# Attention's background product and the branch products in another orientation: weights stationary, 512 and 256 tokens moving, and merged rows kept feature by token

## The chip, the cores and the metric

The kernel runs on one core of one Trainium2 chip. The metric is device time in microseconds (us), the median of several executions. The engines are named as in the profile: PE (TensorE, with its weight loads as PEld), ACT (ScalarE), DVE (VectorE), POOL (GpSimd) and SP (SyncE, which here only issues DMAs).

## What is computed

Two sequences (512 and 256 tokens, width 1024) go through two layers and a last RMSNorm. The kernel treats them as 768 tokens, six tiles of 128. The reference, cut to what matters:

```python
def layer(x, ...):
    h = rmsnorm(x, norm_g)
    proj = h @ w_in
    qa, ka, va, gfl, gbl, za, qb, kb, vb, zb, ma, mb = jnp.split(proj, split_points(), axis=-1)
    ya = gla_branch(qa, ka, va, gfl, gbl, za, ..., w_branch_a)   # (o * silu(za)) @ w_branch_a
    yb = attn_branch(qb, kb, vb, zb, ..., w_branch_b)            # (o * silu(zb)) @ w_branch_b
    merged = jax.nn.sigmoid(ma) * ya + jax.nn.sigmoid(mb) * yb
    return x + merged @ w_out
```

`ma`, `mb`, `ya`, `yb` and `merged` are all 768 x 1024. The change touches these five alone.

## The kernel before

Every dense product runs in three passes of type fp32r: each operand is split into a high part and a low part, and PE adds high x high, high x low and low x high in PSUM. A contraction of 1024 is eight blocks of 128 (`KT` = 8, index `k`). Weights come block by block through a ring of four slots: SP loads `w_raw`, ACT writes the high part `w_hi` (`split`, L992), POOL writes the low part `w_lo` (L1460), and PE waits for `w_lo_done` before a block and signals `w_used` after it. ACT splits three blocks ahead. PE's program is written out by hand, and semaphores order the engines.

The stages of a layer that matter here, in PE's order:

1. **Attention** (`attention_group`), four groups of 20 steps. A step `n` turns the probabilities of one unit on PE (four transposes, `turn_p`, L838), issues the scores of unit `n + 2` (L827, L828), sometimes the product with the values (L852, L853), and turns of queries (L813) in three steps of a group: 3, 6 and 8, in the first group 3, 6 and 11. After such a step `turn_p` waits for `q_stack`, which ACT (L1178) and DVE (L1859) set once both parts of these queries are written. The rest of the step is filled by `background`: pieces of `h @ w_in` for `ma` and `mb`. One group does two pieces of 256 output columns, 16 blocks of 6 token tiles, so 96 tiles (`BG_TILES`). The table `ATT_TILES` says how many tiles each step takes, and `ATT_DONE` is its running sum. One tile is three matmuls with 128 tokens of `act` stationary and 256 columns of the weights moving (L635 to L637). Results stand in banks 5 to 7. ACT copies them to `stg` (L1007) and stores them to the DRAM tensor `proj`.
2. **Four branch products** (`gemm_tokens`, with `three_passes`, L589 to L591): `w_branch_a` with columns 0 to 511, then 512 to 1023, and `w_branch_b` likewise. Each is 8 blocks x 6 token tiles x 3 matmuls = 144 matmuls with 128 tokens stationary and 512 weight columns moving. Token tile `t` has bank `t`. A product takes along six turns (`turn_step`, four transposes of 128x128 and a wait for a free bank 6 or 7, L719). In the first they are of `va`, in the second and third of `zb`, in the fourth of the first half of `merged`.
3. **Merging**: DVE multiplies each bank with the sigmoid factor (`merge`, L1790), and for branch B adds both branches (L1795). The factors come from `proj` by `fetch`, and ACT applies the sigmoid. The sum has tokens on the partitions, but the output product wants features there. So PE turns `merged`, ACT copies the high part out of PSUM into `o_hi` (`turn_hi`, L1049), and DVE writes the low part `o_lo` (`turn_lo`, L1625).
4. **Output product** (`gemm_output`), twice 144 matmuls of the same form for tokens 0 to 383 and 384 to 767. The first takes along the six turns of the second half of `merged`, and waits at block `k` = 4 until they are written.

Of the kernel before, what the change touches and what calls it, by code (L numbers as in the profile page):

```python
# [33 lines left out]
F32 = mybir.dt.float32  # L34
# [6 lines left out]
P = 128  # L41
# [73 lines left out]
ATT_DONE = [[first + sum(tiles[:n + 1]) for n in range(GROUP * UNITS)] for first, tiles in zip(ATT_FIRST, ATT_TILES)]  # L115
ATT_PIECE = [done.index(KT * NT) for done in ATT_DONE]
# [106 lines left out]
class Semaphores:  # L223


    def __init__(self, nc):
# [72 lines left out]
        self.merged_ready = sem("merged_ready")  # L299
        self.zb_ready = sem("zb_ready")  # L300
# [28 lines left out]
def trunk(nc, x_prompt, x_sample, norm_g, w_in, w_gate_f, b_gate_f, w_gate_b, b_gate_b, gla_norm_g,  # L329
# [33 lines left out]
    ma = sb("ma", [P, NT, D], R_ACT)  # L363
    zb = sb("zb", [P, NT, D], R_ACT + NT * D * 4)
    mb = sb("mb", [P, NT, D], R_ACT + NT * D * 4)
    b_lo = sb("b_lo", [P, NT, D], R_M, F32R)
    merged = sb("merged", [P, NT, D], R_V)
# [101 lines left out]
    with nc.Block() as block:  # L469

        @block.sync
        def _(sp):
# [15 lines left out]

            def fetch_inputs(layer, c):
# [17 lines left out]
            def fetch_ma(k):  # L507

                if k == 0:
                    sp.wait_ge(s.stored, at.peek("stored", NBG * 16))  # L510
                if k < 4:
                    fetch(ma, J_MA + k, k * BGW, D, s.m_in[k // 2])

            def fetch_mb(layer, k):
# [3 lines left out]
                if k < 4:  # L518
                    fetch(mb, J_MB + k, k * BGW, D, s.m_in[k // 2])
# [64 lines left out]
        def _(pe):  # L584
# [8 lines left out]
            def gemm_tokens(a_hi, a_lo, turns=None, first=0, half_free=True, after=None, enter=None):  # L593


                for k in range(KT):
                    pe.wait_ge(s.w_lo_done, at("w_lo_done"))
                    if k == KT // 2 and not half_free:
                        pe.wait_ge(s.turn_free, at.peek("turn_free", 2))
                    for t in range(NT):  # L600
                        if k == 0:
                            pe.wait_ge(s.drained, at.peek("drained", t + 1 - NT))
                            if enter:
                                enter(t)
# [4 lines left out]
                        if turns and first <= k < first + 3 and t in (2, NT - 1) and (k, t) != (KT - 1, NT - 1):  # L609
                            turns(2 * (k - first) + t // 3)  # L610
                    (last if k < KT - 1 else pe.drain()).then_inc(s.w_used, 1)
                    if after:
                        after(k)
                at.skip("drained", NT)

            def background(start, stop, bank0=BG_BANK, spare=0, ends=False, turned=0):


                for u in range(start, stop):
# [20 lines left out]
                    elif ends and k == KT - 1 and t % 2 == 1:  # L640
                        last.then_inc(s.bg_done, 1)

# [79 lines left out]

            def merged_step(half):

                def step(t):
                    pe.wait_ge(s.merged_ready, at("merged_ready"))
# [1332 lines left out]
```

## Time and profile before

| what | value |
|---|---|
| median of 3 runs | 1930.85 us (1930.23 to 1932.38) |
| the profiled execution's own time | 1933.38 us |
| its span, first to last instruction | 1931.0 us |
| PE busy | 1882.5 us, 97% of the span |
| DVE, ACT, POOL busy | 987.7, 944.0, 682.8 us (51%, 49%, 35%) |
| granted PE clock | 0.997 of full speed over the span |

A busy PE is not PE at its peak: a matmul's duration as printed (289 ns for 256 columns) reaches past the start of the next. What one matmul costs in a row of them is the distance from its start to the start of the next, which the timeline shows.

### The profile page before, as it was taken

What the parts mean: (1) busy time and instruction counts of PE and PEld (TensorE: products, weight loads), DVE (VectorE), ACT (ScalarE), POOL (GpSimd) and SP (SyncE); (2) the same over time, 40 slices, a digit from 0 to 9 for tenths busy, and PEclk for the clock granted to TensorE, in tenths of its full rate; (3) what the DMA queues carried; (4) which work ended last, traced back from release to release, by engine and by line L of the source; (5) the groups of instructions that cost most, each with busy time, mean ns of one, the idle gap of its engine ahead of it and who ended that gap; (6) DMA issues with size and microseconds to landing.
All of it is one profiled execution on the core that took longest, in us unless ns stands there. A gap on an engine that the chain in (4) does not pass through costs nothing.

```text
span 1931.0 us, 38149 instructions
## 1 busy us (share of the span) xinstructions
PE 1882.5 (97%) x14864; PEld 1728.9 (90%) x14864; DVE 987.7 (51%) x1376; ACT 944.0 (49%) x1891; POOL 682.8 (35%) x688
## 2 busy tenths in 40 slices
PE   6999999999999999999999999999999999999997
PEld 6989999999999999888899899999999999988886
DVE  5113566669655554443241145657886655543324
ACT  4214555532776675423441245555337766763334
POOL 3433233258222122424653333222771221232244
PEclk9999999999999999999999999999999999999999
DMA  5322222522112114332432122225221121261323
GB/s 177 85 58 59 72 78 61 180 82 59 56 48 66 47 50 152 130 126 71 134 104 71 47 65 75 66 76 181 79 58 45 47 67 53 67 208 60 126 93 142
DMA packets 122988, 169.90 MB, mean 88 GB/s; under 512 B 15696, under 2 KB 89296, under 8 KB 122832
## 3 DMA queue, kind: packets, MB, share of 16 engines
q1 hardware_dynamic: 110880, 135.83, 23.7%
q10 hardware_dynamic: 11952, 31.86, 4.3%
q8 instruction: 113, 1.85, 0.4%
q14 instruction: 43, 0.35, 0.1%
HBM read 136.19 MB, written 31.46 MB: 87 GB/s over the span
## 4 chain that ended last, share of the span: by engine, by line
PE 89%; DVE 4%; ACT 3%; issue 3%; ACTq 1%; DMA 0%; POOL 0%; DVEq 0%
PE ps L635 12%; PE ps L636 12%; PE ps L637 12%; PE ps L589 11%; PE ps L591 11%; PE ps L590 11%; PE ps L799 4%; PE ps L838 3%; PE ps L719 2%; PE ps L852 2%; PE ps L853 2%; PE ps L827 2%; PE ps L784 2%; PE ps L828 2%; PE ps L766 1%
## 5 line engine op out<-in xcount | busy, mean ns | idle before, releaser
L1460 POOL TENSOR_TENSOR w_lo<-w_raw,w_hi 128x256 fp32r<-128x256 f32 (+1 forms) x560 | 581.4, 1045 | 1203.9 <-ACT w_hi L992 1202.8
L635 PE MATMUL ps<-w_hi,act_hi 128*128 128x256 f32 x2112 | 610.3, 289 | 6.5 <-ACT stg L1007 5.3
L637 PE MATMUL ps<-w_hi,act_lo 128*128 128x256 f32 x2112 | 597.2, 283 | 0.0
L636 PE MATMUL ps<-w_lo,act_hi 128*128 128x256 f32 x2112 | 597.1, 283 | 0.0
L992 ACT ACTIVATE w_hi<-w_raw 128x256 fp32r<-128x256 f32 (+1 forms) x560 | 273.5, 495 | 507.2 <-PE ps L591 284.2
L635 PEld LDWEIGHTS ps<-w_hi,act_hi 128*128 128x128 f32 x2112 | 403.8, 191 | 14.7 <-issue 9.6
L636 PEld LDWEIGHTS ps<-w_lo,act_hi 128*128 128x128 f32 x2112 | 404.4, 191 | 2.2
L637 PEld LDWEIGHTS ps<-w_hi,act_lo 128*128 128x128 f32 x2112 | 404.2, 191 | 0.0
L1868 DVE TENSOR_REDUCE st<-ps 128x1 f32<-128x512 f32 (+1 forms) x160 | 109.9, 691 | 126.6 <-PE ps L828 126.1
L589 PE MATMUL ps<-w_hi,o_hi 128*128 128x512 f32 x384 | 154.5, 402 | 1.7 <-DVE mb L1790 0.5
L591 PE MATMUL ps<-w_hi,o_lo 128*128 128x512 f32 x384 | 150.2, 391 | 0.0
L590 PE MATMUL ps<-w_lo,o_hi 128*128 128x512 f32 x384 | 149.8, 390 | 0.0
L1188 ACT ACTIVATE pr<-ps,st 128x512 f32<-128x512 f32 (+1 forms) x192 | 117.2, 612 | 12.0 <-DVE st L1868 9.7
L1874 DVE TENSOR_TENSOR pt_lo<-ps,pt_hi 128x512 fp32r<-128x512 f32 x128 | 88.2, 689 | 60.5 <-ACT pt_hi L1198 59.1
L1109 ACT ACTIVATE scaled<-scaled 128x768 f32<-128x768 f32 x64 | 53.2, 831 | 119.7 <-DVE scaled L1726 116.8
L1198 ACT ACTIVATE pt_hi<-ps 128x512 fp32r<-128x512 f32 x128 | 76.6, 599 | 65.9 <-PE ps L853 51.4
L838 PE MATMUL ps<-ident,pr 128*128 128x128 f32 x640 | 96.7, 273 | 7.8 <-DVE q_hl L1859 7.0
L1742 DVE COPY_PREDICATED amat<-mask,ps 128x768 f32<-128x768 uint8 x56 | 58.2, 1040 | 60.7 <-issue 48.3
L589 PEld LDWEIGHTS ps<-w_hi,o_hi 128*128 128x128 f32 x384 | 72.2, 188 | 19.1 <-issue 3.6
L589 PE MATMUL ps<-act_hi,w_hi 128*128 128x384 f32 x256 | 86.2, 337 | 0.5 <-DVE qk_t L1671 0.5
L591 PEld LDWEIGHTS ps<-w_hi,o_lo 128*128 128x128 f32 x384 | 72.1, 188 | 15.6
L591 PE MATMUL ps<-act_hi,w_lo 128*128 128x384 f32 x256 | 85.6, 334 | 0.0
(183 smaller groups left out, 3383.9 us busy)
## 6 DMA issues: line engine op xcount, KB each, us to landing
w_raw<-in_w_in SPq DMA_DIRECT2D x352, 128.0 KB, 2.1
proj<-stg ACTq DMA_DIRECT2D x36, 768.0 KB, 3.5
w_raw<-in_w_in SPq DMA_DIRECT2D x80, 256.0 KB, 2.7
w_raw<-in_w_out SPq DMA_DIRECT2D x64, 256.0 KB, 2.6
w_raw<-in_w_branch_a SPq DMA_DIRECT2D x32, 256.0 KB, 3.0
w_raw<-in_w_branch_b SPq DMA_DIRECT2D x32, 256.0 KB, 2.6
q<-proj SPq DMA_DIRECT2D x8, 768.0 KB, 8.8
zb<-proj SPq DMA_DIRECT2D x8, 768.0 KB, 9.5
```

The source lines that it names most:

```text
L589: mm(out, s_hi, m_hi, start=first, stop=False)
L590: mm(out, s_hi, m_lo, start=False, stop=False)
L591: return mm(out, s_lo, m_hi, start=False, stop=last)
L635: mm(out, act_hi[:, k, tok], w_hi[:, k % RING, 0:BGW], start=(k == 0 and t % 2 == 0), stop=False, skip_group_check=True)
L636: mm(out, act_hi[:, k, tok], w_lo[:, k % RING, 0:BGW], start=False, stop=False, skip_group_check=True)
L637: last = mm(out, act_lo[:, k, tok], w_hi[:, k % RING, 0:BGW], start=False, stop=(k == KT - 1), skip_group_check=True)
L838: last = nc.tensor.transpose(bank(pt_bank(n))[:, place * P:(place + 1) * P], pr[:, n % 2, j * P:(j + 1) * P], ident[:])
L992: A(w_hi[:, slot, 0:width], w_raw[:, slot, 0:width], ACT.Copy).then_inc(s.w_hi_done, 1)
L1188: last = A(pr[:, n % 2, i * w:(i + 1) * w], ps[:, n % 2 * HALF + i * w:n % 2 * HALF + (i + 1) * w], ACT.Exp, bias=nmax(n, i), accum_out=de ...
L1460: G.tensor_tensor(w_lo[:, slot, 0:width], w_raw[:, slot, 0:width], w_hi[:, slot, 0:width].bitcast(F32), ALU.subtract).then_inc(s.w_lo_done, 1)
L1868: V.tensor_reduce(out, view_ps(n % 2 * HALF, (HALF // k, k), (1, HALF // k)), AX.X, ALU.max, negate=True).then_inc(s.neg_max, 1)
L1874: V.tensor_tensor(p_turned(n, True), src, p_turned(n, False).bitcast(F32), ALU.subtract).then_inc(s.pt_lo_ready, 1)
```

## The change

Three things move.

- The attention background becomes `gate_background`. For each block two chunks of 128 weight columns are stationary, and the 768 tokens move. The six places of 256 PSUM columns remain, now (chunk, 256 tokens). Places 0 and 1, and places 4 and 5, lie in one bank and belong to one chunk, and are one matmul of 512 columns where they fall in one step. `ATT_DONE` is moved by one where a step would end inside such a pair.
- The branch products become `gemm_branch`: per block four chunks of 128 weight columns stationary, for each chunk one matmul group of 512 tokens and one of 256. Two chunks share three banks.
- `ma`, `mb` and `merged` are kept feature by token. So the turns of `merged` fall away. ACT makes `o_hi` and DVE `o_lo` straight from `merged` in SBUF (`merged_high`, `merged_low`), and PE waits for `merged_lo` at blocks 0 and 4 of the first output product. The fetches of `ma` and `mb` move one contiguous run of 6 KB per partition (`fetch_features`).

```diff
+ATT_DONE = [[u + (u % NT in (1, 5)) for u in done] for done in ATT_DONE]
...
-    ma = sb("ma", [P, NT, D], R_ACT)
+    ma = sb("ma", [P, KT, TOK], R_ACT)
...
+            def gate_background(start, stop):
+                u = start
+                while u < stop:
+                    i, t = divmod(u, NT)
+                    k = i % KT
+                    n = 2 if t in (0, 4) and u + 2 <= stop else 1
+                    if t == 0:
+                        pe.wait_ge(s.w_lo_done, at("w_lo_done"))
+                    if k == 0 and t % 2 == 0:
+                        pe.wait_ge(s.bg_free, at.peek("bg_free", 1))
+                        at.skip("bg_free", 1)
+                    out = ps[:, BG_BANK * HALF + t * BGW:BG_BANK * HALF + (t + n) * BGW]
+                    col = slice(t // 3 * P, (t // 3 + 1) * P)
+                    tok = slice(t % 3 * BGW, (t % 3 + n) * BGW)
+
+                    mm(out, w_hi[:, k % RING, col], act_hi[:, k, tok], start=(k == 0 and t % 2 == 0), stop=False, skip_group_check=True)
+                    mm(out, w_hi[:, k % RING, col], act_lo[:, k, tok], start=False, stop=False, skip_group_check=True)
+                    last = mm(out, w_lo[:, k % RING, col], act_hi[:, k, tok], start=False, stop=(k == KT - 1), skip_group_check=True)
+                    t += n
+                    u += n
...
+            def gemm_branch(m_hi, m_lo, turns=None, first=0, half_free=True, after=None, enter=None):
+                pieces = [(c, piece) for c in range(4) for piece in range(2)]
+                for k in range(KT):
+                    pe.wait_ge(s.w_lo_done, at("w_lo_done"))
...
+                    for c, piece in pieces:
+                        at0 = piece * (HALF if c % 2 == 0 else BGW)
+                        n = HALF if piece == c % 2 else BGW
+                        flat = c * TOK + at0
+                        b = flat // HALF
+                        opens = flat % HALF == 0
+                        if k == 0 and opens:
+                            pe.wait_ge(s.drained, at.peek("drained", b + 1 - NT))
...
+                        out = ps[:, flat:flat + n]
+                        col = slice(c * P, (c + 1) * P)
+                        mm(out, w_hi[:, k % RING, col], m_hi(k, at0, n), start=(k == 0 and opens), stop=False, skip_group_check=True)
+                        mm(out, w_hi[:, k % RING, col], m_lo(k, at0, n), start=False, stop=False, skip_group_check=True)
+                        last = mm(out, w_lo[:, k % RING, col], m_hi(k, at0, n), start=False, stop=(k == KT - 1), skip_group_check=True)
...
+                        if turns and first <= k < first + 3 and piece == 1 and c % 2 == 1:
+                            turns(2 * (k - first) + c // 2)
...
-                    if first == 0 and k == KT // 2 and c == 0:
-                        pe.wait_ge(s.turn_free, at.peek("turn_free", 2))
+                    if first == 0 and k % (KT // 2) == 0 and c == 0:
+                        pe.wait_ge(s.merged_lo, at("merged_lo", NT))
...
+                b_parts = ((lambda k, at0, n: b_hi[k // (KT // 2)][:, k % (KT // 2), at0:at0 + n]),
+                           (lambda k, at0, n: view(b_lo, at0 // P * D + k * P, (D, n // P), (1, P))))
...
-                gemm_tokens(*b_parts, half_of(zb, 1), half_free=False)
-                gemm_tokens(*b_parts, merged_step(0), first=1)
-                pe.wait_ge(s.turn_free, at.peek("turn_free", 2))
...
+                gemm_branch(*b_parts, half_of(zb, 1), half_free=False)
+                gemm_branch(*b_parts)
+
+                gemm_output(0, OUT_BANKS[0], OUT_FREE[0], lambda i: None)
...
+            def merged_high(half, b):
+                act.wait_ge(s.merged_ready, at("merged_ready"))
+                start = half * (NT * HALF) + b * HALF
+                A(view(o_hi, start, (1, HALF)), view(merged, start, (1, HALF)), ACT.Copy).then_inc(s.merged_hi, 1)
...
-                    if i < NT:
-                        turn_hi(o_hi, i, i, 4)
+                    if 1 <= i <= NT:
+                        merged_high(1, i - 1)
...
+            def merged_low(g):
+                for b in range(NT):
+                    start = g * (NT * HALF) + b * HALF
+                    dve.wait_ge(s.merged_hi, at("merged_hi"))
+                    V.tensor_tensor(view(o_lo, start, (1, HALF)), view(merged, start, (1, HALF)),
+                                    view(o_hi, start, (1, HALF)).bitcast(F32), ALU.subtract).then_inc(s.merged_lo, 1)
```

On PE, step 0 of the second attention group, four background tiles between the scores (L828, now L879) and the next turn of probabilities (L838, now L889). In a row the moving tile stands first behind the arrow, and the columns of the output last. Before:

```order
L828 MATMUL ps<-k_ll,q_hl 128x512
L635 MATMUL ps<-w_hi,act_hi 128x256
L636 MATMUL ps<-w_lo,act_hi 128x256
L637 MATMUL ps<-w_hi,act_lo 128x256
L635 MATMUL ps<-w_hi,act_hi 128x256
L636 MATMUL ps<-w_lo,act_hi 128x256
L637 MATMUL ps<-w_hi,act_lo 128x256
L635 MATMUL ps<-w_hi,act_hi 128x256
L636 MATMUL ps<-w_lo,act_hi 128x256
L637 MATMUL ps<-w_hi,act_lo 128x256
L635 MATMUL ps<-w_hi,act_hi 128x256
L636 MATMUL ps<-w_lo,act_hi 128x256
```

Now:

```order
L879 MATMUL ps<-k_ll,q_hl 128x512
L659 MATMUL ps<-act_hi,w_hi 128x512
L660 MATMUL ps<-act_lo,w_hi 128x512
L661 MATMUL ps<-act_hi,w_lo 128x512
L659 MATMUL ps<-act_hi,w_hi 128x256
L660 MATMUL ps<-act_lo,w_hi 128x256
L661 MATMUL ps<-act_hi,w_lo 128x256
L659 MATMUL ps<-act_hi,w_hi 128x256
L660 MATMUL ps<-act_lo,w_hi 128x256
L661 MATMUL ps<-act_hi,w_lo 128x256
L889 MATMUL ps<-ident,pr 128x128 x4
```

Twelve matmuls of 256 columns became three of 512 and six of 256; the columns are the same.

On PE inside a branch product, before in the fourth around a turn of `merged` (L719), from one token tile to the next:

```order
L589 MATMUL ps<-w_hi,b_hi_66 128x512
L590 MATMUL ps<-w_lo,b_hi_66 128x512
L591 MATMUL ps<-w_hi,b_lo 128x512
L719 MATMUL ps<-ident,merged 128x128 x4
L589 MATMUL ps<-w_hi,b_hi_66 128x512
L590 MATMUL ps<-w_lo,b_hi_66 128x512
L591 MATMUL ps<-w_hi,b_lo 128x512
```

Now, in the second, around a turn of `zb` (L777), which remains:

```order
L777 MATMUL ps<-ident,zb 128x128 x4
L689 MATMUL ps<-o_hi,w_hi 128x512
L690 MATMUL ps<-o_lo,w_hi 128x512
L691 MATMUL ps<-o_hi,w_lo 128x512
L689 MATMUL ps<-o_hi,w_hi 128x256
L690 MATMUL ps<-o_lo,w_hi 128x256
L691 MATMUL ps<-o_hi,w_lo 128x256
L689 MATMUL ps<-o_hi,w_hi 128x256
L690 MATMUL ps<-o_lo,w_hi 128x256
L691 MATMUL ps<-o_hi,w_lo 128x256
L689 MATMUL ps<-o_hi,w_hi 128x512
```

The turns of `merged` have no successor, the others stand twice a block as before, and a block of 18 matmuls has become one of 24.

## Rows read from the trace of the kernel before

**Rows 1.** The page: busy time of each engine, share of the span, instructions

```profile
PE 1882.5 (97%) x14864; PEld 1728.9 (90%) x14864; DVE 987.7 (51%) x1376; ACT 944.0 (49%) x1891; POOL 682.8 (35%) x688
```

**Rows 2.** Windows, layer 0: attention, branch products; PE, PEld, DVE, ACT, POOL, clock, DMA

```profile
497.10:755.40 258.30, 253.75 (x2002) 242.59 (x2001) 148.95 (x251) 183.39 (x448) 52.77 (x70) 1.00 0.18 54
755.40:899.40 144.00, 143.15 (x673) 117.22 (x672) 53.26 (x71) 54.42 (x73) 47.99 (x33) 1.00 0.41 135
```

**Rows 3.** Timeline of PE, 12 matmuls of background in attention: start, duration in us

```profile
559.95 0.28 PE L635 MATMUL ps<-w_hi,act_hi 128*128 128x256 f32 x1
...
561.27 0.28 PE L637 MATMUL ps<-w_hi,act_lo 128*128 128x256 f32 x1
```

**Rows 4.** Timeline of PE, ten matmuls with 512 weight columns moving

```profile
1102.26 0.39 PE L590 MATMUL ps<-w_lo,act_hi 128*128 128x512 f32 x1
...
1104.30 0.39 PE L590 MATMUL ps<-w_lo,act_hi 128*128 128x512 f32 x1
```

**Rows 5.** Timeline of PE, eight matmuls, weights stationary, 384 tokens moving

```profile
51.96 0.33 PE L589 MATMUL ps<-act_hi,w_hi 128*128 128x384 f32 x1
...
53.18 0.33 PE L590 MATMUL ps<-act_lo,w_hi 128*128 128x384 f32 x1
```

**Rows 6.** Timeline of PE, first and last matmul of four products of 144

```profile
97.09 0.47 PE L589 MATMUL ps<-w_hi,act_hi 128*128 128x512 f32 x1 [0.26 <-DVE qk_t L1949]
129.98 0.39 PE L591 MATMUL ps<-w_hi,act_lo 128*128 128x512 f32 x1
...
863.67 0.47 PE L589 MATMUL ps<-w_hi,b_hi 128*128 128x512 f32 x1 [0.26 <-DVE mb L1790]
899.06 0.39 PE L591 MATMUL ps<-w_hi,b_lo 128*128 128x512 f32 x1
...
1850.52 0.47 PE L589 MATMUL ps<-w_hi,o_hi 128*128 128x512 f32 x1 [0.26 <-DVE mb L1790]
1886.31 0.39 PE L591 MATMUL ps<-w_hi,o_lo 128*128 128x512 f32 x1
1886.81 0.49 PE L589 MATMUL ps<-w_hi,o_hi 128*128 128x512 f32 x1
1919.78 0.40 PE L591 MATMUL ps<-w_hi,o_lo 128*128 128x512 f32 x1
```

**Rows 7.** Timeline, second group: turns after steps 3 and 6, and DVE's queries

```profile
569.53 0.28 PE L637 MATMUL ps<-w_hi,act_lo 128*128 128x256 f32 x1
570.37 0.63 PE L838 MATMUL ps<-ident,pr 128*128 128x128 f32 x4 [0.55 <-DVE q_hl L1859]
...
578.24 0.28 PE L637 MATMUL ps<-w_hi,act_lo 128*128 128x256 f32 x1
578.51 0.30 PE L838 MATMUL ps<-ident,pr 128*128 128x128 f32 x1
...
569.36 0.86 DVE L1859 TENSOR_TENSOR q_hl<-ps,q_hl 64x256 fp32r<-64x256 f32 x2
```

**Rows 8.** Timeline of PE, first group: the turns of steps 4 and 19, values in 10

```profile
508.06 0.63 PE L838 MATMUL ps<-ident,pr 128*128 128x128 f32 x4 [0.20 <-DVE q_hl L1859]
...
525.82 0.36 PE L852 MATMUL ps<-ps_hi,v_hl 128*128 128x256 f32 x1 [0.15 <-DVE q L1883]
...
547.40 0.66 PE L838 MATMUL ps<-ident,pr 128*128 128x128 f32 x4 [0.29 <-ACTq L1190]
```

**Rows 9.** Timeline, starts of output products: DVE's products and sums, POOL's low parts

```profile
896.16 4.02 DVE L1790 TENSOR_TENSOR mb<-ps,mb 128x512 f32<-128x512 f32 x6 [11.70 <-PE ps L591]
900.10 5.88 DVE L1795 TENSOR_TENSOR merged<-merged,mb 128x512 f32<-128x512 f32 x6
...
1854.51 1.73 POOL L1460 TENSOR_TENSOR w_lo<-w_raw,w_hi 128x512 fp32r<-128x512 f32 x1 [1.77 <-ACT w_hi L992]
1857.03 1.29 POOL L1460 TENSOR_TENSOR w_lo<-w_raw,w_hi 128x512 fp32r<-128x512 f32 x1 [0.79 <-ACT w_hi L992]
```

**Rows 10.** Line L784, small products in GLA: duration ns min/median/max

```profile
L784 PE MATMUL ps<-scaled x2304: 191/197/270, 184.2 to 1328.9; 128*32 128x32 f32 x160, 128*64 128x64 f32 x32
```

More of the change, by code:

```diff
@@ L299, in __init__ @@
         self.merged_ready = sem("merged_ready")
+        self.merged_hi = sem("merged_hi")
+        self.merged_lo = sem("merged_lo")
         self.zb_ready = sem("zb_ready")
@@ L591, in three_passes, with gemm_tokens @@
                 return mm(out, s_lo, m_hi, start=False, stop=last)
-            def gemm_tokens(a_hi, a_lo, turns=None, first=0, half_free=True, after=None, enter=None):
+            def gemm_tokens(a_hi, a_lo, after):
                 for k in range(KT):
                     pe.wait_ge(s.w_lo_done, at("w_lo_done"))
-                    if k == KT // 2 and not half_free:
-                        pe.wait_ge(s.turn_free, at.peek("turn_free", 2))
                     for t in range(NT):
@@ L608, in gemm_tokens, with background @@
                             last.then_inc(s.gemm_ready, 1)
-                        if turns and first <= k < first + 3 and t in (2, NT - 1) and (k, t) != (KT - 1, NT - 1):
-                            turns(2 * (k - first) + t // 3)
                     (last if k < KT - 1 else pe.drain()).then_inc(s.w_used, 1)
-                    if after:
-                        after(k)
+                    after(k)
                 at.skip("drained", NT)
-            def background(start, stop, bank0=BG_BANK, spare=0, ends=False, turned=0):
+            def background(start, stop, bank0=BG_BANK, spare=0, turned=0):
                 for u in range(start, stop):
@@ L639, in background @@
                         last.then_inc(s.w_used, 1)
-                    elif ends and k == KT - 1 and t % 2 == 1:
-                        last.then_inc(s.bg_done, 1)
+            def gate_background(start, stop):
[17 more added lines that the diff above has]
+                    u += n
+                    if t == NT:
+                        last.then_inc(s.w_used, 1)
+                    elif k == KT - 1 and t % 2 == 0:
+                        last.then_inc(s.bg_done, 1)
@@ L721, in turn_step @@
                 last.then_inc(s.turned, 1)
-            def merged_step(half):
-                def step(t):
-                    pe.wait_ge(s.merged_ready, at("merged_ready"))
-                    turn_step(merged[:, t, half * HALF:(half + 1) * HALF], t)
-                return step
             def half_of(src, half):
@@ L860, in attention_group @@
                     scores(n)
-                background(18 if g == 0 else 0, ATT_FIRST[g])
+                gate_background(18 if g == 0 else 0, ATT_FIRST[g])
                 for n in range(total):
@@ L1408, in _ @@
                     if 1 <= k < 4:
-                        for t in (2 * k - 2, 2 * k - 1):
-                            turn_hi(o_hi, t, t)
+                        for b in (2 * k - 2, 2 * k - 1):
+                            merged_high(0, b)
                     if k == 4:
@@ L1427, in _ @@
                     if i == 0:
+                        act.wait_ge(s.merged_lo, at("merged_lo", 2 * NT))
                         load_norm(norm_g if ahead else final_norm_g, (layer + 1) * D if ahead else 0, layer + 1)
@@ L2002, in _ @@
                 merge(0, True)
-                turn_lo(o_hi, o_lo, tiles)
+                merged_low(0)
                 merge(1, True)
-                turn_lo(o_hi, o_lo, tiles, 4)
+                merged_low(1)
                 residuals(0, OUT_BANKS[0])
```

76 lines of the change are left out of this document (40 added, 36 removed).

## Prediction

> **What bounds the kernel now.** I read the page first: PE is busy in 97% of the span, the next engine in 51% [rows 1]. An average can hide a stage with another limit, so the windows come next: in attention and in the branch products of layer 0 PE is busy for 253.75 of 258.30 us and 143.15 of 144.00 us, at granted clock 1.00 (2.4 GHz), while ACT, the next busiest, has 183.39 and 54.42 us [rows 2]. So PE's instruction stream sets the end in both stages that the change touches. But a matmul's printed duration overlaps its successor's, so the cost has to be read from starts. In the timeline twelve 256-column matmuls start within 1.32 us, 0.120 us apart (11 distances) [rows 3], and ten 512-column ones within 2.04 us, 0.227 us apart (9 distances) [rows 4]. At 2.4 GHz the columns alone take 0.107 and 0.213 us. **Each matmul thus costs its columns plus 0.013 us.** The change keeps all columns, and trades in the number of matmuls.
>
> **Part 1, background in attention.** A block was 18 matmuls of 256 (2.160 us) and is now six of 512 and six of 256 (1.362 + 0.720 = 2.082 us): 0.078 us less. There are 16 blocks x 4 groups x 2 layers = 128: **-10.0 us** of PE work. That it holds with weights stationary and tokens moving is seen at 384 columns, 1.22 us for 7 distances, so 0.174 us, where columns and 0.013 make 0.173 [rows 5].
>
> Not all of it reaches the end. PE waits in attention in some steps, and there less background only means a longer wait. After steps 3, 6 and 8 of a group (3, 6 and 11 in the first) the next turn of probabilities waits for the queries' low parts. After step 3 the starts are 0.84 us apart where 0.12 is usual, 0.55 of it shown as idle, right behind DVE's last write of `q_hl` at 570.22 (569.36 + 0.86); after step 6 they are 0.27 apart, 0.15 late [rows 7]. These chains run through ACT and DVE, start at the turn of the queries, ahead of the step's background, and do not get shorter. So the block of background in each of these steps saves nothing: 24 such waits, 22 of them behind six tiles, 22 x 0.078 = **+1.7 us**. In each layer's first group three tiles change their step because `ATT_DONE` is rounded up to a pair. Step 3 goes from 7 to 8 tiles (2.52 to 2.76 us): its wait, idle 0.20 and about 0.16 more that the overlap hides as in [rows 7], shrinks by 0.24. Step 9 goes from 3 to 4 tiles, which covers the wait of the values in step 10 (0.15 + 0.16 idle and hidden, so -0.3). Step 18 goes from 3 to 2 tiles ahead of the turn in step 19, which already waits 0.29 + 0.16 for the exponential [rows 8]: +0.36. Together about -0.15 per layer, **-0.3 us**. Bounds for all waits together: 0 if ACT and DVE are released earlier too, and the whole 10.0 us if every step waits for its chain. I take +1.4, since each of these waits is seen and most other steps show none.
>
> **Part 2, branch products.** A block was 18 matmuls of 512 (4.086 us) and is now 12 of 512 and 12 of 256 (2.724 + 1.440 = 4.164): 0.078 us more, in 8 blocks x 4 products x 2 layers = 64: **+5.0 us**. Nothing covers it, as PE never waits there but for the hand-over between products [rows 6]. That hand-over stays: bank 5 is still the last to be read out, and the next product opens bank 1 after 0.68 us, bank 2 after 1.40 (was 1.36), against DVE's 0.67 us per bank (4.02 for six) [rows 9]. The one new form is the moving `b_lo`: its tokens lie in runs of 128 with gaps, 256 matmuls with 98,304 columns in all. Cost bounds: nothing, or half speed, 98,304 x 0.417 ns = 41 us. I take nothing: the moving operands of L784 come in runs from 32 down to single elements, and 2304 of them take 191 to 197 ns up to the median [rows 10]. Those are plain fp32 and 32 or 64 columns wide, so it isn't proof.
>
> **Part 3, the turns of merged.** 12 per layer go, six in the fourth branch product, six in the first output product. Their price is read from whole products of 144 matmuls, between first and last start: 32.89 us without turns, 35.39 us with six, so 0.417 us a turn; in the output product 32.97 against 35.79 us, 0.470 a turn [rows 6]. 12 x 0.417 + 12 x 0.470 = **-10.6 us**. Bounds: 24 times either price, -10.0 or -11.3. Here the Trainium skill (TensorE: Matmul & The Clock Gate, Part 4, PE-mode transpose) gives about 0.275 us per transpose in a kernel; 96 of them would be 26 us, and the sum would come out near -30. The products with and without turns decide against adding such durations up.
>
> What replaces the turns lies on ACT and DVE. ACT copies 512 elements per row from SBUF instead of PSUM, DVE subtracts with both inputs in SBUF. PE needs the second six low parts at block 4 of the output product. That comes after 8 half blocks of 9 x 0.227 = 2.04 us, 16.3 us after its start, formerly 2.8 us later. ACT does one `merged_high` behind each of splits 1 to 6, and split 6 waits for half block 5 to be used: 12.3 us, plus 0.4 for the matmul's end and semaphore, 0.6 and 0.6 for split and copy, up to 1.0 for DVE. 14.9 us, so 1.4 us of slack. The sums are ready long before: the six end at 905.98, 6.9 us after the fourth product's last matmul began at 899.06 [rows 6, 9]. If this cover were gone, PE would wait by the excess twice in the run.
>
> **DMAs.** Eight fetches per layer, 768 KB each, become one run of 6 KB per partition instead of six of 1 KB; the queue SP keeps its order and none is on PE's path: 0.
>
> **Sum.** -10.0 + 1.4 + 5.0 - 10.6 = **-14.2 us**. The profiled execution took 1933.38 us (span 1931.0), so 1919.2; the median of the runs lies 2.5 us below it: 1930.85 - 14.2 = **1916.7 us**. What a measurement can tell from no change is 0.2%, 3.9 us.
>
> **Rivals.**
> *A. Attention absorbs its saving.* If most steps turn out bound by the chain scores, maximum, exponential, turn, the 10.0 us become waits: -5.6 us, 1925.3. For it: ACT is 71% busy there. Against: the PE rows of most steps follow each other at 0.12. Chance 0.06.
>
> *B. The 0.013 us is not per matmul* but belongs to something else that stays, and the counts don't matter: only the turns count, -10.6, 1920.3. Against: 256, 384 and 512 columns all fit one constant [rows 3 to 5]. Chance 0.04. The Trainium skill (same page, section "Wait — 56ns, not 53.3ns?") puts the fixed cost at about 2.5 ns per matmul. By that a block of background would save 15 ns and part 1 and 2 together 1 us, and the sum would be near -11.5; the rows show 13 ns, and they decide.
>
> *C. POOL's low parts come late; slower.* `merged_low` gives DVE two SBUF inputs, as its sums have. Beside these sums POOL's `w_lo` takes 1.73 us instead of 1.29 and a sum 0.98 where its products out of PSUM take 0.67 [rows 9]. If POOL stood still for each of the 24 new subtractions, and PE had no slack, that would be 24 x 0.98 = 23.5 us, and the kernel would take 1940.2. It decides once a block's low part takes longer than its block: 1.73 against 2.04 us in the output product and 4.16 in the fourth, with three blocks split ahead. That is why 0.03. The Trainium skill (SBUF — State Buffer, Who interferes with whom) speaks against the change here: a DVE instruction with two SBUF inputs contends with a GpSimd one that reads SBUF, and the loser blocks. The trace agrees on the contention, at 0.44 us.
>
> *D. The gapped b_lo streams at half speed:* +41 us, 1957.7. It eats the gain from 0.144 ns per column on (14.2 us / 98,304). Chance 0.02.
>
> *E. The change does less than it says,* as where a step's end splits pairs: the rounding leaves none split. Under 0.02, ending near no change.
>
> **How the numbers follow.** The forecast has 0.83. Its low end: waits cost nothing more (-10.0 - 0.3), branch +5.0, turns -11.3, with 1 us for the runs' spread: -17.6, 1913.3. Its high end: waits eat 4, turns only -10.0, branch +5.5 and 1 us of spread: -8, some 1922.5; this takes in B. A, C, D and E stay outside, 0.13, and to leave out no more than 0.2 I set 1912.5 to 1922.5. Faster: forecast, A and B, 0.93; within 0.2%: E, 0.02; slower: C and D, 0.05.
>
> **What would show it.** Starts of 512-column background matmuls 0.227 apart and of the others 0.12; a branch product without turns of 8 x 4.16 = 33.3 us between first and last start, with six turns 35.8 to 36.0; the first output product near 33.0; the waits after steps 3, 6 and 8 each some 0.08 longer; ACT's and DVE's new rows at 0.6 and 0.7 to 1.0 us, POOL's at up to 1.7 beside them. It is wrong if PE idles at the first `merged_lo` wait or at block 4 of the output product, if matmuls on `b_lo` are further apart than those on `b_hi`, or if steps of attention without a query turn begin to wait.

## Result, and the profile after

Median of five runs each: before 1930.97 us (1930.23 to 1932.38), changed 1922.16 us (1920.95 to 1922.24). The ratio is 0.9948, with a 95% interval of 0.9937 to 0.9959, so between 7.9 and 12.2 us were gained. The forecast was 1916.7 us, a gain of 14.2. The sign was right, but the size lies above the interval: the ratio itself stands for 10.0 us, so the forecast was 4.2 us too large.

The page, busy time of each engine, share and instructions, answers to [rows 1]:

```profile
PE 1869.9 (97%) x14384; PEld 1691.8 (88%) x14384; DVE 1002.5 (52%) x1376; ACT 943.9 (49%) x1891; POOL 682.3 (36%) x688
```

PE has 480 matmuls fewer and is still the bound. DVE carries 15 us more: its 24 new subtractions take 1.21 us each on average, where the old ones out of PSUM took 0.69, and the 24 sums beside POOL went from 0.89 to 0.99.

Windows of layer 0, the stretches of [rows 2], attention and branch products (PE, PEld, DVE, ACT, POOL, clock, DMA). In both kernels the attention window opens some 10 us behind the start of the stage (the first turn of queries, at 487.07 us before and 485.93 now) and leaves out its first tiles:

```profile
495.95:751.95 256.00, 250.65 (x1639) 220.85 (x1637) 148.95 (x251) 183.23 (x448) 52.49 (x70) 1.00 0.18 55
751.95:896.30 144.35, 143.39 (x841) 124.59 (x840) 55.35 (x71) 54.28 (x73) 46.75 (x33) 1.00 0.39 135
```

Attention lost 2.30 us of its 258.30 and the branch products gained 0.35. In attention PE was busy 3.10 us less, but the span shrank by only 2.30: 0.8 us became idle time.

From the starts of the first instruction of each stage in both traces (own spans 1931.0 and 1920.0 us, of executions that took 1933.38 and 1922.24 us):

| Stage | Forecast, both layers | Layer 0 | Layer 1 | Sum |
|---|---|---|---|---|
| Attention | -8.6 | -2.29 | -2.22 | -4.5 |
| Branch products, six turns gone | 0.0 (+5.0 - 5.0) | +0.34 | +0.18 | +0.5 |
| First output product, six turns gone | -5.6 | -2.87 | -2.88 | -5.75 |
| All else | 0 | -1.25 | 0 | -1.25 |

The last line is, but for 0.1 us, what runs ahead of the first attention, and the change doesn't touch it. Against the kernel before, its length moved by -0.2 to -2.5 us in layer 0 and by 0.0 to +1.0 us in layer 1 over the kernels of this study, whatever was edited. The three lines above it make -9.75 us. So experiments are read below by their stages, and totals only by their intervals.

Timeline of PE, ends of the fourth branch product, of the first output product, and the start of the second, which answer to [rows 6]:

```profile
862.51 0.47 PE L689 MATMUL ps<-b_hi,w_hi 128*128 128x512 f32 x1 [0.26 <-issue]
...
895.96 0.39 PE L691 MATMUL ps<-b_hi,w_lo 128*128 128x512 f32 x1
896.61 0.47 PE L597 MATMUL ps<-w_hi,o_hi 128*128 128x512 f32 x1 [0.26 <-DVE mb L1842]
...
929.52 0.40 PE L599 MATMUL ps<-w_hi,o_lo 128*128 128x512 f32 x1
```

The fourth product takes 33.45 us (33.3 expected), the output product 32.91 us (33.0 expected). The three products that still have six turns take 36.11 us instead of 35.38 (35.8 to 36.0 expected). The hand-over is still 0.65 us.

**The pitch where widths alternate.** PE in the fourth product, one cycle of six wide and six narrow matmuls:

```profile
870.29 0.40 PE L689 MATMUL ps<-b_hi,w_hi 128*128 128x512 f32 x1
870.53 0.40 PE L690 MATMUL ps<-b_lo,w_hi 128*128 128x512 f32 x1
...
871.68 0.28 PE L689 MATMUL ps<-b_hi,w_hi 128*128 128x256 f32 x1
871.79 0.28 PE L690 MATMUL ps<-b_lo,w_hi 128*128 128x256 f32 x1
...
872.39 0.40 PE L689 MATMUL ps<-b_hi,w_hi 128*128 128x512 f32 x1
```

Six wide ones take 1.39 us instead of 6 x 0.227 = 1.362, six narrow ones 0.71 instead of 0.72. By nanoseconds the wide distances are 234, 236, 228, 232, 231, 227, the first narrow one 113, then 119 and 120. A block costs 2.10 us in place of 2.082.

**Attention, second group.** Timeline of PE and DVE at the turns after steps 3 and 6, which answer to [rows 7]:

```profile
567.94 0.28 PE L661 MATMUL ps<-act_hi,w_lo 128*128 128x256 f32 x1
568.81 0.63 PE L889 MATMUL ps<-ident,pr 128*128 128x128 f32 x4 [0.59 <-DVE q_hl L1920]
...
576.46 0.39 PE L661 MATMUL ps<-act_hi,w_lo 128*128 128x512 f32 x1
576.92 0.63 PE L889 MATMUL ps<-ident,pr 128*128 128x128 f32 x4
...
567.81 0.86 DVE L1920 TENSOR_TENSOR q_hl<-ps,q_hl 64x256 fp32r<-64x256 f32 x2
```

The idle time at the first grew from 0.55 to 0.59, and behind step 6 the two starts are 0.46 apart where 0.227 is usual, so the wait there is 0.23 instead of 0.15. Behind steps 3 and 8 the distance grew by 0.04 (0.83 to 0.87 and 0.82 to 0.86), where the forecast had 0.08 for each. Steps 3, 6 and 8 kept their lengths of 4.05, 3.43 and 4.04 us (now 4.05, 3.45, 4.04): what the background saved in them is lost, as forecast.

**Attention, first group.** Timeline of PE at the turns of steps 4 to 6 and 19, and of DVE beside the first, which answer to [rows 8]:

```profile
506.84 0.63 PE L889 MATMUL ps<-ident,pr 128*128 128x128 f32 x4
...
508.71 0.60 PE L889 MATMUL ps<-ident,pr 128*128 128x128 f32 x4
...
509.38 0.39 PE L879 MATMUL ps<-k_ll,q_hl 128*128 128x512 f32 x1
509.89 0.36 PE L903 MATMUL ps<-ps_hi,v_hl 128*128 128x256 f32 x1
...
546.10 0.65 PE L889 MATMUL ps<-ident,pr 128*128 128x128 f32 x4 [0.69 <-ACTq L1241]
...
509.32 0.42 DVE L1944 TENSOR_TENSOR q<-ps,o_low 64x256 f32<-64x256 f32 x1
```

The wait of 0.20 at the turn of step 4 is gone. But the values of step 5 start 0.51 us behind the scores, where 0.23 is usual; DVE's sum of the last output (L1944) ends at 509.74, just ahead of them. The view names no wait there; the distance shows it. That a step without a turn of queries begins to wait is one of the signs of being wrong that the prediction had named. The turn of step 19 waits 0.69 instead of 0.29, as forecast.

### The profile page after: what moved, and what is told of

It reads as the page before. It is cut to its first block, busy times and chain, and to the rows that moved or that the text cites. A ratio compares the mean times of both kernels' runs of the same rounds, so it can differ in the third digit from the quotient of the medians.

```text
span 1920.0 us, 37165 instructions
## 1 busy us (share of the span) xinstructions
PE 1869.9 (97%) x14384; PEld 1691.8 (88%) x14384; DVE 1002.5 (52%) x1376; ACT 943.9 (49%) x1891; POOL 682.3 (36%) x688
## 4 chain that ended last, share of the span: by engine, by line
PE 89%; DVE 4%; ACT 3%; issue 3%; ACTq 1%; DMA 0%; POOL 0%; DVEq 0%
PE ps L636 9%; PE ps L637 8%; PE ps L638 8%; PE ps L597 7%; PE ps L599 6%; PE ps L598 6%; PE ps L689 4%; PE ps L690 4%; PE ps L691 4%; PE ps L660 4%; PE ps L659 4%; PE ps L661 4%; PE ps L850 4%; PE ps L889 3%; PE ps L903 2%
## 5 line engine op out<-in xcount | busy, mean ns | idle before, releaser
L636 PE MATMUL ps<-w_hi,act_hi 128*128 128x256 f32 x1344 | 389.0, 289 | 6.1 <-ACT stg L1052 4.8
L637 PE MATMUL ps<-w_lo,act_hi 128*128 128x256 f32 x1344 | 380.0, 283 | 0.0
L638 PE MATMUL ps<-w_hi,act_lo 128*128 128x256 f32 x1344 | 380.0, 283 | 0.0
L636 PEld LDWEIGHTS ps<-w_hi,act_hi 128*128 128x128 f32 x1344 | 257.2, 191 | 11.4 <-issue 8.4
L637 PEld LDWEIGHTS ps<-w_lo,act_hi 128*128 128x128 f32 x1344 | 257.6, 192 | 0.2
L638 PEld LDWEIGHTS ps<-w_hi,act_lo 128*128 128x128 f32 x1344 | 257.4, 192 | 0.0
L659 PE MATMUL ps<-act_hi,w_hi 128*128 128x512 f32 (+1 forms) x512 | 177.3, 346 | 0.5 <-ACT stg L1052 0.5
L660 PE MATMUL ps<-act_lo,w_hi 128*128 128x512 f32 (+1 forms) x512 | 173.2, 338 | 0.0
L661 PE MATMUL ps<-act_hi,w_lo 128*128 128x512 f32 (+1 forms) x512 | 172.5, 337 | 0.0
L889 PE MATMUL ps<-ident,pr 128*128 128x128 f32 x640 | 96.6, 273 | 9.4 <-DVE q_hl L1920 7.0
L660 PEld LDWEIGHTS ps<-act_lo,w_hi 128*128 128x128 f32 x512 | 97.0, 190 | 8.5
L889 PEld LDWEIGHTS ps<-ident,pr 128*128 128x128 f32 x640 | 75.3, 140 | 25.6 <-issue 13.0
```

The source lines that it names most:

```text
L636: mm(out, act_hi[:, k, tok], w_hi[:, k % RING, 0:BGW], start=(k == 0 and t % 2 == 0), stop=False, skip_group_check=True)
L637: mm(out, act_hi[:, k, tok], w_lo[:, k % RING, 0:BGW], start=False, stop=False, skip_group_check=True)
L638: last = mm(out, act_lo[:, k, tok], w_hi[:, k % RING, 0:BGW], start=False, stop=(k == KT - 1), skip_group_check=True)
L659: mm(out, w_hi[:, k % RING, col], act_hi[:, k, tok], start=(k == 0 and t % 2 == 0), stop=False, skip_group_check=True)
L660: mm(out, w_hi[:, k % RING, col], act_lo[:, k, tok], start=False, stop=False, skip_group_check=True)
L661: last = mm(out, w_lo[:, k % RING, col], act_hi[:, k, tok], start=False, stop=(k == KT - 1), skip_group_check=True)
```

## Experiments

Groups of attention are told by the distance of their first turns. In layer 0 the first took 60.94 us before and 60.69 now, the second 66.04 and 65.33.

**1. Pairs not joined.** The tiles keep their new orientation and the rounded table, but every tile is 256 columns wide.

```diff
-                    n = 2 if t in (0, 4) and u + 2 <= stop else 1
+                    n = 1
```

> The changed kernel with every background matmul in attention 256 columns wide (weights stationary as before, no pair joined; steps as rounded). Theory (each matmul costs its columns plus 0.013 us, and a switch between 512 and 256 columns costs about 0.02 us per block): a block takes 2.160 us instead of 2.101, which is hidden in the steps that wait for queries, so a group of the second to fourth (turn to turn, 65.33 us) takes 66.0 to 66.1, the whole kernel +6 us. By the sum of the prediction (0.078 a block) a group would take 66.4 and the kernel +8.6. Rival (the shortfall comes from the rounding of the steps, and joining pairs is worth its full 0.078): the group 66.4 as well, and so longer than the 66.04 of the kernel before; if the joining is worth nothing, 65.3.

Measured: 1927.61 us, ratio to before 0.9978 (0.9968 to 0.9988). Second group and the turn of its step 4, timeline of PE:

```profile
558.20 0.60 PE L889 MATMUL ps<-ident,pr 128*128 128x128 f32 x4
...
569.51 0.30 PE L889 MATMUL ps<-ident,pr 128*128 128x128 f32 x1 [0.55 <-DVE q_hl L1920]
...
624.23 0.60 PE L889 MATMUL ps<-ident,pr 128*128 128x128 f32 x4
```

The group takes 66.03 us, as the theory had it, and the wait is back at 0.55. In its first group step 5 has the same new wait (0.28 us, 2.44 us long instead of 2.09), so that wait comes from the rounding of `ATT_DONE` and not from wider matmuls. From its first turn to its end attention takes 257.42 us here and 257.45 in the kernel before: all of its gain lies in joined pairs, and the new orientation alone costs nothing.

**2. Branch products in matmuls of 256 columns only.**

```diff
-                pieces = [(c, piece) for c in range(4) for piece in range(2)]
+                pieces = [(c, piece) for c in range(4) for piece in range(3)]
...
-                        at0 = piece * (HALF if c % 2 == 0 else BGW)
-                        n = HALF if piece == c % 2 else BGW
+                        at0 = piece * BGW
+                        n = BGW
```

> The changed kernel with 256 tokens moving in every matmul of the four branch products (three pieces per chunk, 36 matmuls a block instead of 24). Theory (0.013 us per matmul): a block 4.32 us, the fourth product 34.5 us from first to last start (changed kernel 33.45), the kernel about +8.5 us. Rival (the 0.013 us is not per matmul): the fourth product 32.7 to 33.5, the kernel the same or 5 us faster.

Measured: 1928.90 us, ratio 0.9986 (0.9976 to 0.9996). First and last matmul of the fourth product:

```profile
864.90 0.36 PE L689 MATMUL ps<-b_hi,w_hi 128*128 128x256 f32 x1 [0.26 <-issue]
...
899.40 0.28 PE L691 MATMUL ps<-b_hi,w_lo 128*128 128x256 f32 x1
```

34.50 us for 288 matmuls and the same columns, as the theory had it, against 33.45 for 192. The difference of 1.05 us for 96 matmuls is 0.011 each, with the surcharge for alternating widths (experiment 3) gone at the same time; against a product of 144 with one width (32.52 us, see below) it is 0.0138 each. So the price of some 0.013 us per matmul holds, and rival B falls: by it the product would not have grown. The Trainium skill (TensorE: Matmul & The Clock Gate, "Wait — 56ns, not 53.3ns?") has about 2.5 ns per matmul; the trace does not agree.

**3. Widths grouped in the branch products.** In blocks 1 to 6 all wide matmuls of a block come in a row, then all narrow ones, and the next block in the opposite order.

```diff
-                    for c, piece in pieces:
+                    order = pieces
+                    if 0 < k < KT - 1:
+                        wide = [p for p in pieces if p[1] == p[0] % 2]
+                        narrow = [p for p in pieces if p[1] != p[0] % 2]
+                        order = wide + narrow if k % 2 else narrow + wide
+                    for m, (c, piece) in enumerate(order):
```

> The changed kernel with the eight pieces of blocks 1 to 6 of a branch product ordered by width, wide ones first in odd blocks and narrow ones first in even blocks: per product 3 switches to 512 columns and back in these blocks instead of 12. Nothing else moves. Theory (the extra sits in the switch, 0.020 us a cycle): 9 cycles less, the fourth product 33.27 us instead of 33.45, the kernel -1.4 us. Rival (each 512-column matmul with weights stationary is 0.004 us dearer, wherever it stands): 33.45, no change.

Measured: 1923.02 us, ratio 0.9954 (0.9937 to 0.9971). Timeline of PE, the fourth product's first and last matmul, and in it the end of 24 narrow ones and the wide ones behind:

```profile
863.07 0.47 PE L694 MATMUL ps<-b_hi,w_hi 128*128 128x512 f32 x1 [0.26 <-issue]
...
872.82 0.28 PE L696 MATMUL ps<-b_hi,w_lo 128*128 128x256 f32 x1
872.94 0.40 PE L694 MATMUL ps<-b_hi,w_hi 128*128 128x512 f32 x1
...
874.33 0.39 PE L694 MATMUL ps<-b_hi,w_hi 128*128 128x512 f32 x1
...
875.69 0.39 PE L694 MATMUL ps<-b_hi,w_hi 128*128 128x512 f32 x1
...
896.33 0.39 PE L696 MATMUL ps<-b_hi,w_lo 128*128 128x512 f32 x1
```

The product takes 33.26 us. The first six wide matmuls behind narrow ones take 1.39 us, the next six 1.36, which is the old pitch of 0.227. So the surcharge belongs to the change of width and not to the new orientation or to `b_lo`. From 16 stretches of wide matmuls to 7 the product lost 0.19 us, 0.02 each. The three products with turns did not gain as a whole (35.98, 36.36 and 36.32 us against 36.11), and the stage stayed the same, where the expectation had -1.4 us. In the second and third of them two of the six turns, which now stand behind narrow matmuls, start 0.24 us behind the last of these, where 0.12 is usual, and their second transpose comes 0.165 to 0.169 us after the first instead of 0.109. Why they start late is open.

**4. Widths alternating** in threes over blocks 1 to 6, timed once.

```diff
+                        order = [p for both in zip(wide, narrow) for p in both]
```

> The changed kernel with the pieces of blocks 1 to 6 alternating, three matmuls of 512 columns and three of 256: twice as many switches. Theory (the extra sits in the switch): the fourth product 33.45 plus 12 cycles of up to 0.020 us, 33.55 to 33.69. Rival (dearer by form): 33.45.

Measured: 1922.28 us, the fourth product 33.45 us, unchanged. The expectation missed: twice as many changes cost the same in sum. The 33.45 us are what its rival had said (each wide matmul dearer by its form), but the 0.227 us behind the first six in experiment 3 rule that out. A triple of wide ones carries only its own first distances (233, 236, 228 ns), not the whole 0.03 us. The surcharge is spread over the five wide matmuls behind the change, and is no fixed sum.

**5. Tiles of the later groups moved** into steps 3 and 8, behind whose background the turn waits for `q_hl`, out of steps 0 and 1, which don't wait. The other entries that differ only write down what the rounding of `ATT_DONE` makes of the old ones.

```diff
-    (4, 4, 2, 6, 2, 2, 6, 2, 6, 3, 3, 2, 4, 6, 3, 3, 6, 3, 6, 5),)
+    (2, 2, 2, 8, 2, 2, 6, 2, 8, 4, 2, 2, 4, 6, 4, 2, 6, 4, 6, 4),)
```

> The changed kernel with only the table of the second to fourth attention group altered: two background tiles each go from steps 0 and 1 (4 to 2) to steps 3 and 8 (6 to 8), where PE waits 0.75 and 0.74 us for the queries after the last background matmul. Theory (those waits are fixed chains and PE has other work to fill them): two tiles take 0.70 us, so a group gets 1.4 us shorter, 65.33 to 63.9, the kernel 6 x 1.4 = -8.4 us. Rival (the steps that give tiles away begin to wait for their exponential, as step 5 of the first group did when it lost a tile): the group 64.6 to 65.3, the kernel 0 to -4.

Measured: 1916.00 us, ratio 0.9914 (0.9897 to 0.9930). Second group, timeline of PE: the first turn, those behind steps 3 and 8, and the third group's first:

```profile
556.18 0.60 PE L889 MATMUL ps<-ident,pr 128*128 128x128 f32 x4
...
565.84 0.40 PE L661 MATMUL ps<-act_hi,w_lo 128*128 128x512 f32 x1
566.11 0.63 PE L889 MATMUL ps<-ident,pr 128*128 128x128 f32 x4
...
581.17 0.63 PE L889 MATMUL ps<-ident,pr 128*128 128x128 f32 x4 [0.18 <-DVE q_hl L1920]
...
620.52 0.60 PE L889 MATMUL ps<-ident,pr 128*128 128x128 f32 x4
```

The group takes 64.34 us, 1.0 less, which lies between the theory (63.9) and its rival (64.6 and more). Behind step 3 the wait is gone. Behind step 8 the two tiles (0.70 us) made the wait only 0.39 us shorter, and the step grew from 4.04 to 4.37. Why, was not tried. Steps 0 and 1 gave 0.71 and 0.66 us and wait for nothing new, so the rival's reason did not appear.

**6. The same move in the kernel before**, with its old orientation.

```diff
-    (4, 4, 2, 6, 2, 2, 6, 2, 6, 3, 3, 2, 4, 6, 3, 3, 6, 3, 6, 5),)
+    (2, 2, 2, 8, 2, 2, 6, 2, 8, 3, 3, 2, 4, 6, 3, 3, 6, 3, 6, 5),)
```

> The kernel before with the same move of two tiles each from steps 0 and 1 to steps 3 and 8 in the second to fourth group. If the gain of moving tiles has nothing to do with the orientation: a group 66.04 to 64.6 (waits of 0.71 and 0.70 us filled by 0.72 us of work), the kernel -8.5 us, near 1922.5.

Measured: 1926.04 us, ratio 0.9963 (0.9951 to 0.9976); the group takes 64.92 us, 1.1 less instead of the 1.4 expected. The waits were there before the change, and filling them is worth about the same in both kernels (1.1 and 1.0 us a group).

**7. Tiles of the first group moved**, two from step 12 to step 11 and two from step 16 to step 18; the other entries again write down the rounding.

```diff
-ATT_TILES = ((2, 2, 2, 7, 1, 2, 6, 2, 4, 3, 3, 6, 3, 3, 2, 2, 3, 2, 3, 2),) + 3 * (
+ATT_TILES = ((2, 2, 2, 8, 0, 2, 6, 2, 4, 4, 2, 8, 2, 2, 2, 2, 2, 2, 4, 2),) + 3 * (
```

> The changed kernel with only the table of the first attention group altered: two tiles from step 12 to step 11, two from step 16 to step 18. In the changed kernel PE waits 0.34 us after step 11 and 0.85 us after step 18. Theory (waits are filled): -0.34 and -0.70, so the first group (turn to turn 60.69 us) 59.65, the kernel -2.1 us. Rival (new waits where the tiles leave): the group 60.3 to 60.7.

Measured: 1921.67 us, ratio 0.9940 (0.9924 to 0.9957). The group takes 59.96 us, 0.73 less instead of 1.0. The waits in steps 11 and 18 are gone, but steps 13 and 14 now wait 0.38 and 0.45 us (before this edit 0 and 0.19): part of the gain moved on.

**8. and 9. Two tiles back into step 4** of the first group, once from step 5, once from step 3; each was timed once.

```diff
-ATT_TILES = ((2, 2, 2, 7, 1, 2, 6, 2,
+ATT_TILES = ((2, 2, 2, 8, 2, 0, 6, 2,
```

> First group of each layer: the two tiles of step 5 run in step 4 instead, between the transposed values and the next turn. Theory (in the changed kernel step 4 has no tile left, so the values of step 5 arrive before DVE has made o_summed, which stands behind its low parts): the wait of step 5 is covered, step 4 grows from 1.87 to about 2.57 us, step 5 shrinks from 2.44 to about 1.4 us, and the group takes 60.3 instead of 60.7 us. Rival (ACT and DVE between two steps are the bound, not this one hand-over): the wait comes back before a turn or before the values of steps 5 to 7, and the group stays at 60.6 to 60.8 us.

```diff
-ATT_TILES = ((2, 2, 2, 7, 1, 2, 6, 2,
+ATT_TILES = ((2, 2, 2, 6, 2, 2, 6, 2,
```

> First group of each layer: two of the eight tiles of step 3 run in step 4, as one did in the kernel before. Theory: the wait of step 5 for o_summed goes (step 5 from 2.44 to 2.09 us), but step 3 is bound by the queries' low parts and does not get shorter (4.05 us, its wait 0.6 us), so step 4 adds its 0.70 us in full: the group takes 61.0 us instead of 60.7. Rival (step 5 waits for something that has nothing to do with the tiles of step 4): step 5 stays at 2.44 us and the group takes 61.4 us.

From step 5, timeline of PE, the turns of steps 5, 6 and 7:

```profile
509.35 0.60 PE L889 MATMUL ps<-ident,pr 128*128 128x128 f32 x4
510.72 0.60 PE L889 MATMUL ps<-ident,pr 128*128 128x128 f32 x4
514.56 0.63 PE L889 MATMUL ps<-ident,pr 128*128 128x128 f32 x4 [0.24 <-DVE q_hl L1920]
```

Step 5 is down to 1.37 us, as the theory had it, but step 6 takes 3.84 us instead of 3.43. Of these 0.41 us about half are at its turn of queries, which starts 0.40 us behind the scores instead of 0.24, and 0.18 at the turn behind it, which waits for `q_hl`. DVE writes the last of `q_hl` 17.6 us after the group's first turn here and 17.5 in the changed kernel. The group stays at 60.69 us, which was the rival. From step 3, the turns of steps 4, 5 and 6:

```profile
506.88 0.63 PE L889 MATMUL ps<-ident,pr 128*128 128x128 f32 x4 [0.58 <-DVE q_hl L1920]
509.45 0.60 PE L889 MATMUL ps<-ident,pr 128*128 128x128 f32 x4
511.54 0.60 PE L889 MATMUL ps<-ident,pr 128*128 128x128 f32 x4
```

Step 5 is at its old 2.09 us and step 4 at 2.57; the group takes 60.92 us (61.0 expected). So the wait of step 5 is indeed one that a tile in step 4 covers, but a second chain, over the queries of step 6, ends just as late. Whole times were 1922.30 and 1922.95 us.

**10. and 11. The moves together**: later groups (5), first group (7), and widths grouped in the product without turns; then the same with step 4 as in 8. Of the first:

```diff
+                    if 0 < k < KT - 1 and not turns:
```

> The changed kernel with both tables, and with the pieces of the fourth branch product (the one without turns) grouped by width. If the parts add up: -8.4 - 2.1 - 0.4 = -10.9 us against the changed kernel, near 1911; with new waits in the steps that give tiles away, 1915.

> The changed kernel with the tiles of the later groups moved, those of the first group moved with two tiles in step 4 from step 5, and the widths grouped in the product without turns. Against the kernel with the first three of these, one wait per layer less: theory 0.3 to 0.4 us less in each first group (59.6 instead of 59.96 us) and the whole at 1915 us; rival: the group stays at 59.9 to 60.0 us.

Measured: 1915.79 us, ratio 0.9908 (0.9891 to 0.9924), and 1914.43 us, ratio 0.9913 (0.9900 to 0.9927). The first came out at the expectation with new waits (1915) and not at the plain sum of its parts (1911). The two can't be told apart, and the first group takes 60.01 and 60.06 us, so the rival held for the second. Both beat the changed kernel, whose interval begins at 0.9937. Nearly all of it is experiment 5, whose ratio is 0.9914. The page of the last one:

```profile
PE 1869.8 (98%) x14384; PEld 1691.9 (88%) x14384; DVE 1000.7 (52%) x1376; ACT 943.9 (49%) x1891; POOL 682.4 (36%) x688
```

PE does the same work as in the changed kernel and is done 7.8 us earlier (spans of 1912.2 and 1920.0 us).

## Why the prediction was right or wrong

**What bounds the kernel: right.** PE's stream set the end in every stage that changed, and the size of the gain was a matter of matmuls saved and waits left.

**Part 1, 0.078 us per block: too large.** This is the main failed step: "six of 512 and six of 256 (1.362 + 0.720 = 2.082 us)" added up two pitches that had each been read from a long uniform stretch. Where six wide and six narrow ones alternate a cycle takes 2.10 us, by the rows above. Over the second group, background alone and waits left out, the 16 blocks went from 34.51 to 33.66 us: 0.053 a block. For 128 blocks this is -6.8 instead of -10.0. In experiment 1, with the new orientation but one width, the same sum is 34.52, and experiment 3 shows in the branch products that the surcharge sits at the change of width.

**Waits: +1.4 forecast, +2.3 measured** (4.5 of 6.8 arrived). In the six later groups each lost 0.21 us of 0.85, together +1.3, most of it in the three waits that were named. The first groups were mis-seen: forecast was that the rounding gains 0.15 us a layer, and that most steps there take their saving to the end. Experiment 1 shows the rounding alone: 60.89 and 60.93 us instead of 60.94 and 60.95, so 0.02 to 0.05 gained. They gained 0.32 and 0.37 us (start of the stage to the second group) of 0.85 each, so the waits took +1.0 for both. The wait behind step 3, that of the values in step 10 and that ahead of the turn in 19 moved as forecast, but the tile moved out of step 4 was taken to cost nothing there: its place was the cover of the sum of outputs on DVE, and steps 3 to 5 together took 8.38 us in both kernels. (The rounding also moves a tile from step 13 to step 12, which the prediction passed over; the two together kept their 4.95 us in experiment 1.) And steps 6, 8, 11, 14 and 18 of this group wait in both kernels, so they kept their lengths to within 0.04 us. The saving of a block had been called lost in only two of them, 6 and 11.

**Part 2 and the turns beside it: right in sum (+0.5 against 0.0), by luck, with two errors that cancel.** The 32.89 us from which the turn was priced is not a product of 144 alone. Between its ends PE also does this, timeline of the kernel before, which [rows 6] pass over:

```profile
117.37 0.39 PE L591 MATMUL ps<-w_hi,act_lo 128*128 128x512 f32 x1
117.60 0.50 PE L742 MATMUL ps<-gl_t,wg_fix 128*128 128x512 f32 x2
117.94 0.40 PE L589 MATMUL ps<-w_hi,act_hi 128*128 128x512 f32 x1
```

Two matmuls of GLA (L742, one of 512 and one of 256 columns) take 0.34 us there, and some 0.03 more go in the recovery behind them. A plain product is 32.52 us. So six turns cost (35.39 - 32.52) / 6 = 0.478 us each in the branch product too, and went for -5.7 in both layers instead of -5.0. Against that, eight blocks without turns grew from 32.52 to 33.45 us, 0.116 a block, and those with turns by 0.73 / 8 = 0.091. That is 2 x (0.93 + 3 x 0.73) = +6.2 instead of +5.0, again the change of width, twice in a block. The sum, +0.5, is the table's. Experiment 2 against the plain product gives (34.50 - 32.52) / 144 = 0.0138 us per matmul.

**Part 3, output product: right,** -5.75 against -5.6. The 24 turns of both places brought 5.7 + 5.75 = 11.5 us. The Trainium skill (TensorE: Matmul & The Clock Gate, Part 4, PE-mode transpose) has about 0.275 us per transpose; an estimate by that figure, 96 times, would be 26 us, and the trace does not agree with the sum. It does agree with the figure as a duration: the 96 transposes of `merged` are printed with 0.272 us each on average, but within a turn they start 0.108 us apart.

**The slack of 1.4 us: right in kind, smaller.** DVE's `merged_low` was put at up to 1.0 us, from a mean of 0.98. That mean hid two values. Timeline of DVE and POOL in the fourth product and behind it:

```profile
871.96 1.29 POOL L1512 TENSOR_TENSOR w_lo<-w_raw,w_hi 128x512 fp32r<-128x512 f32 x1 [2.85 <-ACT w_hi L1037]
...
872.43 1.36 DVE L1855 TENSOR_TENSOR o_lo<-merged,o_hi 128x512 fp32r<-128x512 f32 x1 [2.18 <-ACT o_hi L1107]
...
873.72 0.68 DVE L1855 TENSOR_TENSOR o_lo<-merged,o_hi 128x512 fp32r<-128x512 f32 x1
...
903.78 1.34 POOL L1512 TENSOR_TENSOR w_lo<-w_raw,w_hi 128x512 fp32r<-128x512 f32 x1 [0.36 <-ACT w_hi L1037]
...
903.90 1.77 DVE L1855 TENSOR_TENSOR o_lo<-merged,o_hi 128x512 fp32r<-128x512 f32 x1
...
910.38 1.63 DVE L1855 TENSOR_TENSOR o_lo<-merged,o_hi 128x512 fp32r<-128x512 f32 x1
```

Over all 24 of them, a subtraction that starts while POOL works takes 1.36 to 1.82 us and ends some 0.55 us behind POOL (873.25 to 873.79, 905.12 to 905.67), one that doesn't takes 0.68. The last of the six is done at 912.01. PE's block 4 begins at 896.61 + 16.4 = 913.01, so 1.0 us of the slack was left and PE did not idle there.

**The range.** Its high end does not follow from its own terms. -10.0 + 4 (waits) + 5.5 - 10.0 (turns) + 1 (spread) is -9.5 us, so 1921.4, and not -8. The measured 1922.16 lies beyond what these terms add up to, and inside the stated 1922.5 by luck.

**Rivals.** A: attention did not absorb its saving, two thirds arrived. B: refuted by experiment 2, though its time, 1920.3, was nearer to the measured one than the forecast's. C: the contention is real, but beside the new subtractions POOL's low parts took at most 1.60 us (1.68 beside the sums) against 2.04 per block, and PE waited for none. D: no. In the fourth product, where `b_lo` moves with its gaps, the wide distances are those of the second behind its last turn, where `o_lo` moves without (1.39 us for six in both), and in experiment 3 they fall to 0.227. E: no, the gain is clear of no change.

## What to carry to other kernels

Price a mixture of forms from a stretch of that mixture, or count its changes of form: the pitch of a uniform stretch was a lower bound here. A product used as a measure must be looked through for foreign instructions. When tiles of filler work are shifted between steps, even by one, each step's filler is the cover of some chain; look at which wait it hid before calling the shift free. Where the trace shows that a step waits while its neighbours don't, moving filler into it can be worth more (here six groups x 1.0 us) than making the filler cheaper (4.5 us).

## What the runs showed of the hardware

- A wide matmul behind something else is slower for a while. Behind narrow matmuls, behind a turn or behind a stall the first five to eight of 512 columns come mostly 228 to 236 ns apart, then 226 to 227; the first narrow one behind wide ones comes after 113, then 119 to 120. A change to wide and back costs some 0.02 us net where six stand in a row (experiment 3), and less where three do (experiment 4). The kernel before shows the same distances behind its turns of `merged`. What makes them so was not tried.
- DVE's subtraction with two SBUF inputs (0.68 us alone) and POOL's (1.29 us alone) hold each other up: the one that starts later ends its own work behind the other. DVE's takes up to 1.82 us when it starts second, POOL's 1.60 when it does (905.82, behind DVE's of 905.59). The Trainium skill (SBUF — State Buffer, Who interferes with whom) says that a DVE instruction with two SBUF inputs contends with a GpSimd one that reads SBUF, that the lock is exclusive and that the order of issue decides who blocks. An estimate by that page for a subtraction that meets POOL at its start is 1.29 + 0.68 = 1.97 us. The trace agrees on the order, and nearly on the size: one that starts 0.03 us behind POOL (907.89) takes 1.81 us and ends 0.55 us behind it, not 0.68.
